# The opening of a three-layer transformer kernel: order of its first loads, of scale and shift, of weight casts, and who sums the context's squares

## The reference, cut to what matters

```python
def rms_norm(x, g):
    xf = x.astype(jnp.float32)
    y = xf * lax.rsqrt(jnp.mean(jnp.square(xf), axis=-1, keepdims=True) + EPS)
    return (y * g.astype(jnp.float32)).astype(x.dtype)

def modulate(h, shift, scale):
    return h * (1.0 + scale) + shift

def ada_mod(cvec, w, b):
    return jnp.split(jax.nn.silu(cvec) @ w + b, 6, axis=-1)
...
        sh1, sc1, g1, sh2, sc2, g2 = [t[:, None, :] for t in ada_mod(c, ada_w[i], ada_b[i])]
        h = modulate(rms_norm(x, norm1_g[i]), sh1, sc1)
        if i % 2 == 0 or ctx_needed:
            csh1, csc1, cg1, csh2, csc2, cg2 = ada_mod(c_ctx, ada_w[i], ada_b[i])
            hc = modulate(rms_norm(ctx, norm1_g[i]), csh1, csc1)
        if i % 2 == 0:
            w_in = a_w_in[j]
            u = h @ w_in
            ukc = hc @ w_in[:, Q_LORA:EVEN_KV_END]
...
```

## Time and profile before

| | us |
|---|---|
| runs (3) | 1075.52, 1075.18, 1071.6 |
| median of the runs | 1075.18 |
| span of the profiled execution, first to last instruction | 1073.6 |
| PE busy in that span | 1048.8 |
| DVE busy | 780.6 |
| ACT busy | 552.8 |
| POOL busy | 106.3 |

### The profile page before, as it was taken

The page is one execution under the profiler, slowest core; times in us unless marked ns, Lnnn a source line. Parts: engine busy times, 40 slices in busy tenths (PEclk is TensorE's granted clock), DMA queues, the critical chain, the costliest instruction groups (busy, mean ns, idle before and its releaser), DMA issues.

```text
span 1073.6 us, 20190 instructions
## 1 busy us (share of the span) xinstructions
PE 1048.8 (98%) x7898; PEld 954.2 (89%) x7898; DVE 780.6 (73%) x1381; ACT 552.8 (51%) x951; POOL 106.3 (10%) x125
## 2 busy tenths in 40 slices
PE   7999999999999999999999999999999999999998
PEld 2887687999999989888999999888866799999998
DVE  2687767788888678846676775697539867777876
ACT  4646756444443574655344444545337665554442
POOL 2100004000000027520000000300331010000000
PEclk9999998999999999999999999999999999999999
DMA  9981265898898717465787876386450054546551
GB/s 363 410 328 54 86 243 189 319 363 320 332 346 332 259 60 251 162 240 182 289 286 274 288 264 214 113 313 235 124 111 30 2 195 139 197 161 205 166 191 40
DMA packets 68593, 232.83 MB, mean 217 GB/s; under 512 B 12144, under 2 KB 12432, under 8 KB 68144
## 3 DMA queue, kind: packets, MB, share of 16 engines
q1 hardware_dynamic: 62496, 227.20, 59.3%
q0 software_dynamic: 5888, 3.73, 1.7%
q10 hardware_dynamic: 144, 1.05, 0.3%
HBM read 230.85 MB, written 1.05 MB: 216 GB/s over the span
## 4 chain that ended last, share of the span: by engine, by line
PE 87%; DVE 6%; DMA 2%; issue 2%; ACT 1%; POOL 1%; SPq 0%; DVEq 0%; POOLq 0%; ACTq 0%
PE bank L1882 25%; PE bank L1884 25%; PE bank L1883 25%; PE bank L2401 3%; DMA w_raw<-weights 2%; PE bank L2044 2%; DVE bank L1320 1%; PE bank L1909 1%; PE bank L2053 1%; PE bank L2067 1%; PE bank L1964 1%; DVE w_lo L1193 1%; DMA a_raw<-ada 1%; PE bank L2283 1%; DVE nmax L1327 1%
## 5 line engine op out<-in xcount | busy, mean ns | idle before, releaser
L1882 PE MATMUL bank<-h_hi,w_hi 128*128 128x256 f32 (+2 forms) x1408 | 405.0, 288 | 6.3 <-DVE h_lo L1289 3.7
L1884 PE MATMUL bank<-h_hi,w_lo 128*128 128x256 f32 (+2 forms) x1408 | 402.0, 286 | 0.0
L1883 PE MATMUL bank<-h_lo,w_hi 128*128 128x256 f32 (+2 forms) x1408 | 401.2, 285 | 0.0
L1193 DVE TENSOR_TENSOR w_lo<-w_raw,w_hi 128x1024 fp32r<-128x1024 f32 x271 | 328.9, 1237 | 65.9 <-ACT w_hi L693 64.4
L693 ACT CAST w_hi<-w_raw 128x1024 fp32r<-128x1024 f32 x271 | 275.5, 1045 | 71.0 <-PE bank L1884 59.9
L1882 PEld LDWEIGHTS bank<-h_hi,w_hi 128*128 128x128 f32 x1408 | 267.9, 190 | 15.0 <-issue 9.2
L1883 PEld LDWEIGHTS bank<-h_lo,w_hi 128*128 128x128 f32 x1408 | 268.2, 191 | 1.3 <-issue 0.2
L1884 PEld LDWEIGHTS bank<-h_hi,w_lo 128*128 128x128 f32 x1408 | 268.2, 191 | 1.0
L1884 PE MATMUL bank<-g_hi,w_lo 128*128 128x256 f32 x528 | 148.6, 281 | 0.0
L1882 PE MATMUL bank<-g_hi,w_hi 128*128 128x256 f32 x528 | 148.5, 281 | 0.0
L1883 PE MATMUL bank<-g_lo,w_hi 128*128 128x256 f32 x528 | 148.5, 281 | 0.0
(11 more groups left out here) (208 smaller groups left out, 1239.8 us busy)
## 6 DMA issues: line engine op xcount, KB each, us to landing
w_raw<-weights SPq DMA_DIRECT2D x281, 512.0 KB, 5.0
a_raw<-ada SPq DMA_DIRECT2D x140, 512.0 KB, 5.4
vals<-ada SPq DMA_DIRECT2D x4, 512.0 KB, 8.7
a_raw<-rpb POOLq DMA_DIRECT2D x9, 224.0 KB, 17.1
bias<-rpb POOLq DMA_DIRECT2D x7, 224.0 KB, 7.8
xT<-xt SPq DMA_DIRECT2D x1, 1024.0 KB, 8.8
big<-ctx SPq DMA_DIRECT2D x1, 1024.0 KB, 14.7
big<-ctx ACTq DMA_DIRECT2D x1, 1024.0 KB, 7.0
```

The costliest lines, as they stand in the source:

```text
L1193: nc.vector.tensor_tensor(w_lo[:, s, :], w_raw[:, s, :], w_hi[:, s, :].bitcast(fp), SUB)\
L1882: nc.tensor.matmul(out, a_hi, b_hi, start=start, stop=False)
L1883: nc.tensor.matmul(out, a_hi, b_lo, start=False, stop=False)
L1884: return nc.tensor.matmul(out, a_lo, b_hi, start=False, stop=stop)
```

## The change

Six things are done. (1) The parameters' first 48 columns (the conditions) are loaded by themselves, then the first modulation group, then the selectors, the other parameters and x. (2) Group 3 comes third and goes through `a_raw`, group 1 comes fourth and goes through `vals`; the rows and columns on PE and DVE's order follow. (3) On ACT the shifts of tiles 4 to 7 stand ahead of the cast of w3, and the cast of w2 ahead of the copy of group 1. (4) The tables (864 KB) and the four modulation blocks of the next group are issued two weight blocks later. (5) All eight squares of the context's norm are added on GpSimd, and PE's sum and spread of it stand inside projects 3 and 4. (6) The first sum block of DVE moves from project 3 to project 7's group.

```diff
-ROW_GROUPS = [0, 2, 1, 3, 24, 25, 26, 27]
+ROW_GROUPS = [0, 2, 3, 1, 24, 25, 26, 27]
...
-    at = {RING + n: 17 + n for n in range(4)}
+    at = {RING + 2 + n: 17 + n for n in range(4)}
...
-        POOLED = [8, 4, 5, 4, 5, 7, 4, 5]
+        POOLED = [8, 8, 5, 4, 5, 7, 4, 5]
...
-            sp.dma_start(par[:], params_in).then_inc(s_par, 16)
+            c1 = PARAMS["c"][1]
+            sp.dma_start(par[:, 0:c1], params_in[:, 0:c1]).then_inc(s_cond, 16)
+            ada_to(AGRP)
             sp.dma_start(con[:, 0:N_SELECT], consts_in[:, 0:N_SELECT]).then_inc(s_con, 16)
-            ada_to(AGRP)
+            sp.dma_start(par[:, c1:N_PARAMS], params_in[:, c1:N_PARAMS]).then_inc(s_par, 16)
...
-                if w == RING:
+                if w == RING + 2:
                     sp.dma_start(con[:, N_SELECT:N_CONSTS], consts_in[:, N_SELECT:N_CONSTS]).then_inc(s_tab, 16)
...
-            act.wait_ge(s_par, 16)
+            act.wait_ge(s_cond, 16)
...
+            ada_copy(3)
+            split_to(2)
             ada_copy(1)
-            ada_copy(3)
-            split_to(3)
+            act.wait_ge(mod_ready, 4)
             for k in range(4, KT):
                 shift(0, k)
+            act.wait_ge(s_par, 16)
+            split_to(3)
...
+            ada_take(3)
+            dve.wait_ge(mod_ready, 3)
+            first_gain(4)
+            scale(0, 4)
+            scale(0, 5)
+            split_to(2)
             ada_take(1)
-            ada_take(3)
+            scale(0, 6)
             dve.wait_ge(mod_ready, 4)
-            first_gain(4)
-            norm_tiles(0, 4, KT)
+            shift_low(0, 4)
+            scale(0, 7)
+            for k in range(5, KT):
+                shift_low(0, k)
...
-                sum_mod_blocks((0, 0, 0, 1, 0, 0, 2, 2, 3, 2)[j])
+                sum_mod_blocks((0, 0, 0, 0, 0, 0, 2, 3, 3, 2)[j])
...
-                    project(("in0", j), W_IN0 + j, xs, T)
+                    project(("in0", j), W_IN0 + j, xs, T,
+                            between={3: {5: lambda: norm_sums(1)}, 4: {4: lambda: norm_spread(1)}}.get(j, {}))
...
-                if j == 2:
-                    norm_sums(1)
-                if j == 3:
-                    norm_spread(1)
```

More of the change, by code:

```diff
@@ L61, in splits_to @@
     return w + 1 - sum(n <= w for n in WHOLE)
-ROW_GROUPS = [0, 2, 1, 3, 24, 25, 26, 27]
+ROW_GROUPS = [0, 2, 3, 1, 24, 25, 26, 27]
 SUM_GROUPS = [g for g in range(N_A // AGRP) if g not in ROW_GROUPS]
-STREAM = [0, 2, 1, 3, *range(4, 10), 24, *range(10, 22), 25, 26, 27, 22, 23, *range(28, N_A // AGRP)]
+STREAM = [0, 2, 3, 1, *range(4, 10), 24, *range(10, 22), 25, 26, 27, 22, 23, *range(28, N_A // AGRP)]
 assert N_A % AGRP == 0 and FT % 2 == 0
@@ L322, in program @@
         shift_cols = sb("shift_cols", [P, 4])
+        s_cond = sem("cond_columns_loaded")
         s_par, s_con, s_x, s_ctx = sem("params_loaded"), sem("selectors_loaded"), sem("x_loaded"), sem("ctx_loaded")
@@ L2229, in _ @@
             norm_spread(0)
-            ada_rows(1)
+            ada_rows(3)
             first_products(range(0, 2))
-            ada_rows(3, range(4))
+            ada_rows(1, range(4))
+            ada_columns(3)
+            ada_rows(1, range(4, KT))
+            first_products(range(2, 3))
             ada_columns(1)
-            ada_rows(3, range(4, KT))
-            first_products(range(2, 3))
-            ada_columns(3)
             first_products(range(3, 4))
```

## The result

The changed kernel takes 1080.1 us (median of 8 runs, 1077.72 to 1081.59) against 1075.43 (8 runs, 1071.6 to 1077.81): ratio 1.0049, 95% interval 1.0032 to 1.0066. It is slower by about 5 us, where 1.0 was forecast. The profiled span grew from 1073.6 to 1078.8 us.

What follows compares the result with a forecast made beforehand. It took PE as the bound (98% busy), with DVE full and transfers second. PE's some +0.9 us and DVE's +1.0 meet, the larger counts: +1.0 on the median 1075.18, forecast 1076.2 us, range 1070.5 to 1080.0.

Steps and rivals of the forecast that it cites:

- What bounds the kernel: Whole kernel: PE busy 98% of 1073.6 us, DVE nearly full after 49 us, DMA full from 6 to 57 us.
- First part: Start of the kernel: condition columns and first blocks loaded ahead; PE starts up to 1.0 us sooner, worth 0 us.
- Second part: Start of the second half: scale before shift, shifts before casts; first product at 36.05 instead of 36.32, -0.25 us.
- Third part: Context's eight squares on GpSimd: done at 47.35, PE stands 3.55 us in project 3; +0.9 with the clock.
- The term of the clock: PE after its wait for GpSimd: clock falls until near 49.15, 1.8 us of work at half speed, +0.9 us.
- second rival: PE waits 3.5 us or more for GpSimd's sum, clock low until about 52.6; +2.6 us, 1078.3; chance 0.22.
- the lower end of -3.8: Best case: no PE wait, no clock fall, DVE in time: -0.25 - 1.8 - 0.3 - 1.5 = -3.8 us.
- Fourth part: Tables and first sum block later: next modulation block issued at 61.8, DVE begins rope 2.0 us late; +1.0 us.
- The slack of 0.94 us: Third query tile: its low part ended at 80.89, PE took it at 81.83, so 0.94 us of delay vanishes.
- Both delays meet at 82 us and the larger counts: PE's delay of some 0.9 us and DVE's of 1.0 are put under a maximum, giving +1.0 us.
- the signs named in advance: First 80 us: first addition near 13.2, PE idle 2.5 to 4 us in project 3, low clock near 46 to 49.
- The rival of an early GpSimd: Context's additions end at 44.4, PE waits 0.6 us, clock holds; -0.5 to -3.0 us, 1073.5; chance 0.22.

Runs made afterwards that it cites:

- e7: Kernel before with only the new order of the first loads (condition columns first, other parameters behind the selector); ratio 0.9998 to the kernel before.
- e5: Changed kernel with 16 unused identity products on PE ahead of the sum that waits for GpSimd; ratio 1.0035 to the kernel before.
- e4: Kernel before with only the context's eight squares on GpSimd, PE's sum and spread inside projects 3 and 4; ratio 1.0012 to the kernel before.
- e6: Kernel before with only DVE's first sum block moved later, as in the change; ratio 1.0016 to the kernel before.
- e1: Changed kernel with DVE's first sum block, and the counts of the later groups, put back; ratio 1.0017 to the kernel before.
- e2: Changed kernel with the context's squares, sums and spread put back (four squares on GpSimd); ratio 1.0020 to the kernel before.
- e8: Changed kernel with the modulation block that waits for the first sum issued behind three weight blocks, not ahead; ratio 1.0009 to the kernel before.
- e3: Changed kernel with both DVE's first sum block and the context's squares, sums and spread put back; ratio 1.0005 to the kernel before.
- e10: Changed kernel with DVE's first sum block put back, PE's sums of the squares moved into project 4, spread into project 5; ratio 0.9998 to kernel before.

## Why the prediction was wrong

1. **What bounds the kernel** held: PE's losses and DVE's fill decided, and both came from the first 85 us. A slip without consequence: 0.512/0.410 is 1.25; a block of 512 KB is 0.524 MB, which gives the 1.28 us.
2. **First part, 0 us**: right (e7: 0.9998, marks -0.3).
3. **Second part, -0.25**: the 1.0 us of idle time came (33.87), the product at 36.38 instead of 36.05, since the blocks too landed 0.4 us later. The same product stood between 35.79 and 36.32 in the five kernels without this part and between 35.69 and 37.10 in those with it, so a gain of 0.25 can't be told from nothing.
4. **Third part**: GpSimd was done at 47.49 (47.35 forecast), PE stood 3.50 us (3.55 forecast). The term of the clock was too small: +0.9 for one stretch, and the clock was low for 6.83 us. The end of project 4 is +3.0 against a forecast of about +0.9; e5 puts 2.9 of it on the clock. This is what the second rival (+2.6) said for this part. With one low stretch, in e4, it is +2.0.
 The Trainium skill, "SBUF — State Buffer", section "Who interferes with whom", has the two engines exclude each other for a whole instruction. The trace agrees: an addition took 0.73 us alone and 1.59 beside a subtraction. By the Trainium skill, "TensorE: Matmul & The Clock Gate", section "What's actually happening", the clock falls after idle time; the fall at 47.22 came at the end of the wait, and e5, without the wait, had none.
 One price was wrong and stayed without effect on the sum: the low stretch of before was put at 1.5 us, which the lower end of -3.8 counts as a gain. e6, without it, reaches the sums of project 4 no sooner, since PE then waits for DVE's inverse.
5. **Fourth part**: the issue and the small work of DVE were right where this part stands alone (e6: 62.02 and 80.58, forecast 61.8 and 81.1). The slack of 0.94 us was not there. It was taken at the low part of the third query tile (L1556, ended 80.89), but PE waits for the instruction behind it (L1594 of the kernel before), the first of which ended at 81.7, 0.1 us ahead of PE's start at 81.83; and in e6 PE had waited 1.28 us already for the bank with the gains. So the part costs 2.1 us, not 1.0.
6. **The step that failed is the sum: "Both delays meet at 82 us and the larger counts."** They follow one another.
   - *Why.* The late sum block stands on DVE behind the low parts of project 6, and these wait for PE. So a late PE makes the issue late too: 62.02 in e6 and 61.99 in e5, where project 4 is on time, 64.72 in the changed kernel. The blocks land one behind the other from then on, and DVE's waits of 3.77, 1.33 and 0.29 come on top of PE's delay.
   - *How much.* At the rope part: +3.0 from project 4 and +2.75 from the list make +5.75. Corrected in size, the two terms alone are 2.0 (e4) and 2.1 (e6); the larger would be 2.1 and the sum 4.1, and 5.8 was measured. e1 and e2 say the same from the other side: undo either, and part of the loss stays.
   - *What is above the sum*, 1.6 us, has two sources in the marks: the low clock lasted 6.8 us instead of e4's 3.4 (project 4 at 55.44 for 54.42, 1.0 us), and the third block after the issue landed 2.94 us behind the second instead of e6's 2.09 (0.9 us). No edit explains either, and both may differ in another execution. The times don't show this surplus: their intervals are wider than it.

The range ended at 1080.0 and the median is 1080.1: its upper bound had the worst of one term in it and not both terms one behind the other. The 0.5% that a measurement was said to need was too much: the interval, 0.32% to 0.66%, is clear of no change. Of the signs named in advance two were off: the first addition came at 13.80 instead of 13.2, and the low clock was twice as long and began a little later. The rival of an early GpSimd is refuted by 47.49 in the changed kernel and 47.86 in e4.

Left open: why the clock was low for 6.8 us after a wait of 3.50 and for 3.4 after waits of 1.98 (e1), 2.00 (e8) and 4.15 (e4); what makes the falls near 15, 22, 36 and 46 come in one kernel and not in another; and why x landed 0.8 us sooner in e3, e5 and e8 than in five kernels with the same first loads.

## What to carry to other kernels

Before two delays are put under a maximum, ask whether the second starts from an event that the first moves: a load released by work that stands behind the delayed engine adds its delay to it. An issue in a queue that is served in order costs what stands behind it; look there before an edit gives its release away. And work given to a slower engine is to be asked for as late as the program allows: the same eight squares put x 2.0 us later when they were waited for in project 3, and 1.5 sooner in project 4 (by the marks; neither time is clear of before).

## What the runs showed of the hardware

- A queue that has run empty does not restart evenly. After the late issue the first block took 3.4 to 3.8 us to land and the next 1.2 to 1.3 more, but the third came after 2.94 us in the changed kernel, 2.09 in e6, 1.49 in e5 and 1.29 in e2, at the same order of issues.
- With the first block ahead of all but the condition columns it landed 1.0 us sooner, at 5.07 instead of 6.08. That was not passed on: x, issued some way behind it, landed at 13.0 to 13.1 in the changed kernel, e1, e2, e7 and e10 and at 12.2 to 12.3 in e3, e5 and e8, with the same list of loads; with the old list it landed at 12.3 to 12.8. Such a scatter has to be known before a difference of half a microsecond is read from two profiles.
- Products of no use, issued into a wait of 3.5 us (e5), and no low clock came: the end of project 4 went from 55.44 to 51.90. The four kernels in which PE stood 2.0 to 4.2 us there (changed, e1, e4, e8) all had one at the wait's end or within 2 us of it.
- The clock also fell without idle time of PE, near 46, behind 2.3 us of one-column products: before and in e2, e3 and e7. In e6, with the same products, it did not, so they alone do not bring it.
- A low clock is not always a loss. The 3.4 us of it near 46 cost 1.7 us of PE's pace before, and project 4 ended no later for it, as PE had to wait for DVE's inverse anyway.
